# A rebuilt tail and a 512-column projection in a two-block transformer kernel on one Trainium2 core

## What is computed

```python
def second_block(x, g_mix, w_in, ..., w_e_gate, w_e_up, w_e_down, g_final):
    h = rmsnorm(x, g_mix[l])
    proj = h @ w_in[l]                       # queries, keys, values, gates of two attentions
    ...
    h = rmsnorm(x, g_ffn[l])
    x = x + hier_moe(h, ...)                 # 32 experts, 2 for each token
    return rmsnorm(x, g_final)

def hier_moe(h, ...):
    ...
    for e in range(N_EXPERTS):
        a = jax.nn.silu(hf @ w_e_gate[e]) * (hf @ w_e_up[e])
        out = out + gates[:, e:e + 1] * (a @ w_e_down[e])

def rmsnorm(x, gain):
    y = x32 * lax.rsqrt(jnp.mean(x32 * x32, axis=-1, keepdims=True) + RMS_EPS)
    return (y * gain).astype(x.dtype)
```

## Time and profile before

| | us |
|---|---|
| median of three runs | 1656.29 |
| the profiled execution | 1658.78 |
| its span, from first to last instruction | 1656.9 |
| TensorE busy | 1476.0 (89%) |
| VectorE, ScalarE, GpSimd busy | 766.9, 578.5, 462.3 |
| mean granted clock of TensorE | 0.954 of 2.4 GHz |

### The profile page before, as it was taken

One profiled execution on the slowest core, in us unless ns is written; L12 is line 12 of the kernel. 1 busy time (PEld: TensorE's weight loads), 2 busy tenths in 40 slices (PEclk: granted clock), 3 DMA queues, 4 the chain that ended last, 5 costly groups with the idle time before them and its releaser, 6 DMA issues.

```text
span 1656.9 us, 26936 instructions
## 1 busy us (share of the span) xinstructions
PE 1476.0 (89%) x10612; PEld 1176.3 (71%) x10612; DVE 766.9 (46%) x1476; ACT 578.5 (35%) x965; POOL 462.3 (28%) x257
## 2 busy tenths in 40 slices
PE   7999999999999999999999999999996666676665
PEld 6898998999999699889999998888942221131112
DVE  2665357777774274577776433768720000000002
ACT  2271444444453264444444333656410000000001
POOL 1332424555443142355555444212200000000000
PEclk9999999999999999999999999999998888778887
DMA  7464634555559443455552565243899999999994
GB/s 299 153 219 156 216 110 145 191 188 178 174 183 264 168 166 111 145 192 188 178 190 81 206 217 182 90 180 114 352 424 423 426 424 424 423 426 425 425 425 204
DMA packets 78691, 401.13 MB, mean 242 GB/s; under 512 B 8320, under 2 KB 13056, under 8 KB 67200
## 3 DMA queue, kind: packets, MB, share of 16 engines
q1 hardware_dynamic: 77584, 395.80, 64.6%
q10 hardware_dynamic: 1008, 3.94, 0.6%
HBM read 394.01 MB, written 1.05 MB: 238 GB/s over the span
## 4 chain that ended last, share of the span: by engine, by line
PE 64%; issue 28%; DVE 5%; ACT 1%; POOL 1%; DMA 0%; DVEq 0%; SPq 0%; POOLq 0%; ACTq 0%
PE pw L2097 10%; PE pw L2090 5%; PE pw L2099 5%; PE pw L2091 5%; PE pw L2092 5%; PE acc L2090 5%; PE acc L2091 4%; PE acc L2092 4%; PE pw L2413 4%; PE acc L2104 3%; PE acc L2273 2%; PE pw L2186 1%; PE pw L2235 1%; PE pw L2236 1%; PE pw L2237 1%
## 5 line engine op out<-in xcount | busy, mean ns | idle before, releaser
L1144 POOL TENSOR_TENSOR wl<-raw,wh 128x1024 fp32r<-128x1024 f32 x157 | 384.5, 2450 | 589.6 <-ACT wh L732 586.5
L732 ACT ACTIVATE wh<-raw 128x1024 fp32r<-128x1024 f32 x314 | 329.7, 1054 | 274.5 <-PE pw L2092 106.4
L2097 PE MATMUL pw<-a_pair,wh 128*128 128x512 f32 x720 | 256.8, 399 | 6.2 <-DVE cf L1598 3.3
L1261 DVE TENSOR_TENSOR wl<-raw,wh 128x1024 fp32r<-128x1024 f32 x157 | 203.7, 1298 | 108.9 <-ACT wh L732 108.7
L2099 PE MATMUL pw<-a_pair,wl 128*128 128x256 f32 x720 | 202.2, 281 | 0.0
L2090 PE MATMUL acc<-yh,wh 128*128 128x256 f32 x672 | 192.1, 286 | 0.5 <-DVE wl L1261 0.5
L2091 PE MATMUL acc<-yh,wl 128*128 128x256 f32 x672 | 190.1, 283 | 0.0
L2092 PE MATMUL acc<-yl,wh 128*128 128x256 f32 x672 | 190.1, 283 | 0.0
L2097 PEld LDWEIGHTS pw<-a_pair,wh 128*128 128x128 f32 x720 | 135.4, 188 | 38.4 <-DVE cf L1598 7.2
L2090 PE MATMUL pw<-a_pair,wh 128*128 128x256 f32 x552 | 159.5, 289 | 1.5 <-DVE gt L1770 1.5
L1155 POOL TENSOR_TENSOR small<-small 128x2 f32<-128x2 f32 x12 | 12.1, 1005 | 518.6 <-DVE small L1278 514.2
(11 more groups left out here) (354 smaller groups left out, 2438.6 us busy)
## 6 DMA issues: line engine op xcount, KB each, us to landing
raw<-in_stream SPq DMA_DIRECT2D x358, 512.0 KB, 3.4
raw<-in_experts SPq DMA_DIRECT2D x28, 2048.0 KB, 40.8
ring_w<-in_experts SPq DMA_DIRECT2D x18, 2048.0 KB, 33.4
ring_y<-in_experts SPq DMA_DIRECT2D x28, 1024.0 KB, 35.7
early_e<-in_experts SPq DMA_DIRECT2D x10, 2048.0 KB, 35.9
ring_a<-in_experts SPq DMA_DIRECT2D x10, 2048.0 KB, 36.1
ring_k<-in_experts SPq DMA_DIRECT2D x10, 2048.0 KB, 37.1
ring_b<-in_experts SPq DMA_DIRECT2D x10, 1024.0 KB, 34.0
```

The costliest lines, as they stand in the source:

```text
L732: A.done(act.activation(wh[:, s.base % SPLIT, :], raw[:, slot_of(s.base), :], ACT.Copy), w_hi)
L1144: G.done(pool.tensor_tensor(wl[:, s.base % SPLIT, :], raw[:, slot_of(s.base), :], wh[:, s.base % SPLIT, :].bitcast(F32), ALU.subtract), w_ ...
L1261: V.done(dve.tensor_tensor(wl[:, s.base % SPLIT, :], raw[:, slot_of(s.base), :], wh[:, s.base % SPLIT, :].bitcast(F32), ALU.subtract), w_lo_v)
L2097: pe.matmul(bank[:, 0:2 * T], wh[:, s.base % SPLIT, w], pair, start=start, stop=False, skip_group_check=True)
```

## The change

It has two parts.

In the **projection**, `col_phase` is called with `halves`, so the 29 slabs use `tile2`, and `col_out` scales the two halves (the low one into the scratch tile `t[1]`) and adds them.

In the **tail**, the last step becomes two: the last transfer is issued as two of 1 MB with a semaphore each (`last_in0`, `last_in1`), its weights lie in DRAM by halves, and each half brings what 128 output channels need. There are five steps `u`, with the chunks of `LAST`. Behind the products and the placing of a step `u` from 1 on, TensorE sums the squares of the step before (`out_sums`); VectorE adds two chunks behind the low part of a step (`take_experts`), and ScalarE squares them. The sums use a full 128 x 128 ones matrix and go to `pw2`, so that every partition holds the sums of all tokens. The flag of the branch is loaded ahead of the last steps, and the branch stands behind the additions on VectorE and behind the sums on TensorE; the dense form takes the additions back first. The column product, the copy, the diagonals and the spreading product go: VectorE scales the sums into `parts`, GpSimd raises all 128 x 256 of them to the power -1/2 into `rstd_b`, and the eight last multiplications read that from SBUF in place of PSUM.

```diff
@@ -50,6 +50,7 @@
+LAST = [(0, 2), (2, 4), (4, 6), (6, 7), (7, 8)]
@@ -549,6 +550,18 @@
+        def last_part(u):
+            lo, hi = LAST[u]
+            return pw[lo // 4][:, (lo % 4) * P:(lo % 4 + hi - lo) * P]
+        def last_slab(u, e, k):
+            m, n = EXPERT * QUADS - 4 + min(u, 3), LAST[u][1] - LAST[u][0]
+            if u < 3:
+                return expert_slab(m, e)[:, T * k:T * k + T]
+            return expert_place(m)[:, 2 * (u - 3) + e // 2, 512 * (e % 2) + P * k:512 * (e % 2) + P * k + P]
@@ -693,9 +706,13 @@
-            for m in range(FIRST, len(order)):
+            for m in range(FIRST, len(order) - 1):
+            wait_slab(sp, At(S0["moe"] + left_by(len(order) - 1)))
+            for h in range(2):
+                sp.dma_start(expert_place(len(order) - 1)[:, 2 * h:2 * h + 2, :],
+                             experts[order[-1], :, 2 * h:2 * h + 2, :]).then_inc(S(f"last_in{h}"), 16)
@@ -1071,13 +1088,22 @@
-            def y_hi_last(n):
-                wait_slab(act, At(NSLAB - 4 + n))
-                if n == 0:
+            def y_hi_last(u):
+                if u == 3:
+                    act.wait_ge(S("last_products"), 1)
+                else:
+                    wait_slab(act, At(NSLAB - 4 + min(u, 3)))
+                if u == 0:
-                A.done(act.activation(ye_hi[:, T * n:T * n + T], pw[n // 2][:, T * (n % 2):T * (n % 2) + T], ACT.Copy),
-                       S("expert_out_hi"))
+                lo, hi = LAST[u]
+                A.done(act.activation(ye_hi[:, P * lo:P * hi], last_part(u), ACT.Copy), S("expert_out_hi"))
+            def out_squares(u):
+                for c in range(*LAST[u]):
+                    wait_new_x(act, "moe", c)
+                    A.done(act.activation(sq_late[:, c, :], x[:, c, :], ACT.Square), sq_ready)
@@ -1114,10 +1140,14 @@
-            for n in range(4):
-                y_hi_last(n)
+            for u in range(5):
+                y_hi_last(u)
+                if 1 <= u < 4:
+                    out_squares(u - 1)
+            out_squares(3)
+            out_squares(4)
@@ -1246,7 +1279,9 @@
-            rstd("out")
+            pool.wait_ge(parts_ready, NORMS["out"] + 1)
+            G.fence()
+            G.done(pool.tensor_tensor(rstd_b[:], parts[:], mhalf[:, 0:1].broadcast_to([P, T]), ALU.pow), rstd_ready)
@@ -1337,6 +1369,8 @@
+                elif name == "win" and LEAD <= n < 32:
+                    ins = dve.tensor_tensor(dst, halves_scaled(pw[u % 4], t[1][:], scale), t[1][:], ALU.add)
@@ -2023,11 +2057,19 @@
-            def y_lo_last(n):
-                dve.wait_ge(S("expert_out_hi"), 2 * (QUADS - 1) + n + 1)
-                w = slice(T * n, T * n + T)
-                V.done(dve.tensor_tensor(ye_lo[:, w], pw[n // 2][:, T * (n % 2):T * (n % 2) + T],
-                                         ye_hi[:, w].bitcast(F32), ALU.subtract), S("expert_out_lo"))
+            def y_lo_last(u):
+                dve.wait_ge(S("expert_out_hi"), 2 * (QUADS - 1) + u + 1)
+                w = slice(P * LAST[u][0], P * LAST[u][1])
+                V.done(dve.tensor_tensor(ye_lo[:, w], last_part(u), ye_hi[:, w].bitcast(F32), ALU.subtract),
+                       S("expert_out_lo"))
+            def take_experts(lo):
+                dve.wait_ge(S("scattered"), QUADS - 1 + lo + 2)
+                V.fence()
+                for c in (lo, lo + 1):
+                    V.done(dve.tensor_tensor(x[:, c, :], acc_of(c), x[:, c, :], ALU.add), acc_out)
@@ -2051,11 +2093,18 @@
-            for n in range(4):
-                y_lo_last(n)
+            for u in range(5):
+                y_lo_last(u)
+                if 1 <= u < 4:
+                    take_experts(2 * u - 2)
+            take_experts(6)
+            V.fence()
...
@@ -2070,15 +2119,14 @@
-            V.fence()
-            take_sums("moe")
-            norm_parts("out")
-            norm_mean("out")
-            norm_diag("out")
-            dve.wait_ge(bc_full, spread_no("out"))
-            V.fence()
...
+            dve.wait_ge(stat_full, NORMS["out"] + 1)
+            V.done(dve.tensor_scalar(parts[:], pw[2][:, 0:T], 1.0 / D, EPS, ALU.mult, ALU.add), parts_ready)
+            dve.wait_ge(rstd_ready, NORMS["out"] + 1)
-                V.done(dve.scalar_tensor_tensor(x[:, c, :], x[:, c, :], col("g_final", c), acc[0][:, T:2 * T],
+                V.done(dve.scalar_tensor_tensor(x[:, c, :], x[:, c, :], col("g_final", c), rstd_b[:],
@@ -2484,7 +2532,7 @@
-            col_phase("win", 32 - LEAD, a_pair, spread_at("mix"), final_spread, 5, LEAD, LEAD)
+            col_phase("win", 32 - LEAD, a_pair, spread_at("mix"), final_spread, 5, LEAD, LEAD, True)
@@ -2718,15 +2766,12 @@
-            def scatter(q, chunks=range(KC)):
+            def scatter(q, chunks=range(KC), u=0):
-                if not ending:
-                    pe.wait_ge(S("expert_out_lo"), 2 * q + 2)
+                pe.wait_ge(S("expert_out_lo"), 2 * q + 1 + u if ending else 2 * q + 2)
-                    if ending and c % 2 == 0:
-                        pe.wait_ge(S("expert_out_lo"), 2 * q + 1 + c // 2)
@@ -2735,21 +2780,33 @@
+            def out_sums(u):
+                for c in range(*LAST[u]):
+                    pe.wait_ge(sq_ready, KC * sq_no("out") + c + 1)
+                    ins = pe.matmul(pw[2][:, 0:T], ones[:], sq_late[:, c, :], start=(c == 0), stop=(c == KC - 1))
+                    if c == KC - 1:
+                        ins.then_inc(stat_full, 1)
-                m = EXPERT * QUADS - 4
-                for n in range(4):
-                    wait_expert(pe, At(S0["moe"] + m + n))
+                for u in range(5):
+                    if u < 3:
+                        wait_expert(pe, At(NSLAB - 4 + u))
+                    else:
+                        pe.wait_ge(S(f"last_in{u - 3}"), 16)
-                            ins = pe.matmul(pw[n // 2][CAP * e:CAP * e + CAP, T * (n % 2):T * (n % 2) + T],
-                                            ht_last[:, k, CAP * e:CAP * e + CAP],
-                                            expert_slab(m + n, e)[:, T * k:T * k + T],
-                                            start=(k == 0 and n % 2 == 0), stop=(k == 3), skip_group_check=True)
-                    ins.then_inc(slab_done, 1)
-                    if n == 0:
+                            ins = pe.matmul(last_part(u)[CAP * e:CAP * e + CAP, :], ht_last[:, k, CAP * e:CAP * e + CAP],
+                                            last_slab(u, e, k), start=(k == 0 and u in (0, 2)), stop=(k == 3),
+                                            skip_group_check=True)
+                    ins.then_inc(S("last_products") if u == 3 else slab_done, 1)
+                    if u == 0:
-                    scatter(QUADS - 1, range(2 * n, 2 * n + 2))
+                    scatter(QUADS - 1, range(*LAST[u]), u)
+                    if u >= 1:
+                        out_sums(u - 1)
+                out_sums(4)
@@ -2804,10 +2861,11 @@
+            over = pe.value_load(overflow[0:1, 0:1], min_val=0, max_val=1)
-            over = pe.value_load(overflow[0:1, 0:1], min_val=0, max_val=1)
@@ -2833,9 +2891,10 @@
-            sq_sums("out", src=sq_late)
-            norm_column("out")
-            norm_spread("out")
...
@@ -2973,7 +3032,8 @@
-    experts = np.concatenate([experts, quarters])
+    halves = quarters[3].reshape(P, Q, 4, 2, P).transpose(0, 3, 1, 2, 4).reshape(1, P, Q, SLAB)
+    experts = np.concatenate([experts, quarters[:3], halves])
```

More of the change, by code:

```diff
@@ L1131, in _ @@
                             .then_inc(S("dense_turned"), 1)
-            squares(x, lambda c: wait_new_x(act, "moe", c), into=sq_late)
+                act.wait_ge(stat_full, NORMS["out"] + 1)
+                for c in range(KC):
+                    act.wait_ge(S("dense_added"), c + 1)
+                    act.activation(sq_late[:, c, :], x[:, c, :], ACT.Square).then_inc(S("dense_squares"), 1)
         @block.gpsimd
@@ L2053, in _ @@
             y_lo(QUADS - 2, 1)
-            for n in range(4):
-                y_lo_last(n)
             over = dve.value_load(overflow[0:1, 0:1], min_val=0, max_val=1)
+            for u in range(5):
[4 more added lines that the diff above has]
+            V.fence()
             with dve.If(over > 0):
-                dve.wait_ge(S("scattered"), QUADS - 1 + KC)
+                dve.wait_ge(sq_ready, KC * sq_no("out") + KC)
+                for c in range(KC):
+                    dve.tensor_tensor(x[:, c, :], x[:, c, :], acc_of(c), ALU.subtract).then_inc(S("dense_undone"), 1)
+                dve.wait_ge(S("dense_undone"), KC)
                 for q in range(TT):
@@ L2835, in _ @@
                 last.then_inc(S("dense_down"), 1)
-            sq_sums("out", src=sq_late)
-            norm_column("out")
-            norm_spread("out")
+                pe.wait_ge(S("dense_squares"), KC)
+                for c in range(KC):
+                    last = pe.matmul(pw[2][:, 0:T], ones[:], sq_late[:, c, :], start=(c == 0), stop=(c == KC - 1))
```

(1 more changed line is left out.)

9 lines of the change are left out of this document (5 added, 4 removed).

## The result

The changed kernel took 1692.97 us, the median of four runs (1691.5 to 1694.71), against 1655.78 us for the kernel before: a ratio of 1.023, with a 95% interval from 1.0218 to 1.0242. It is slower by 37 us, and outside the range of the prediction (1648 to 1680 us). The profiled execution took 1691.5 us around a span of 1689.7 us.

A forecast was written before the change was run, and what follows sets the result against it. Limits by stretch: matmuls in the projection, expert weights from 1169 us, a handover chain at the end. Projection -1.6, tail -5.75, power +4.7 give -2.65 us, median 1653.6 us, no measurable change; own range 1651 to 1661, outer range 1648 to 1680.

The forecast's parts named there:

- the price X: Tail: time of GpSimd's power of 256 columns, taken as 4.7 us between 1.4 and 54.
- The column rival: Tail: the power is paid by the column; at X = 27, +19.7 us, 1676 us, slower; chance 27%.
- deciding point of 12.3 us: Tail: the power's time X from which the column rival decides and the forecast of no measurable change fails.
- 0.6 + X: Tail, parts to last multiplications: parts 0.42 us, handovers about 0.18, and the power X, in place of 4.29 us.
- The term of the sums (-2.05 us): Tail: with most additions, squares and sums done before the last low part, the sums end 2.05 us earlier.
- The walk: Tail: turns priced one by one from quarter 1's placing at 1631.35 to the sums' end at 1644.7 us.
- the second transfer would gain no start: Tail: the first half lands 2.4 us earlier, but its products don't start before 1637.45, so no start is gained.
- The projection (-1.6 us): Input projection: 29 slabs, each 0.055 us shorter at 2.825 us in place of 2.88, give -1.6 us.
- should reach the end: From projection to end: what comes off the projection should reach the end, as each later stretch follows the one before.
- VectorE's 0.82 us: Tail, around the branch: VectorE's idle time ahead of the eight additions; moving the branch costed at nothing, at most 0.82 us.
- The clock rival: Tail: the end runs at 1.2 GHz, +3.3 us, 1656.9 us, no change; 5% together with the projection rival.
- VectorE didn't lag: Projection rival: VectorE lags and the 1.6 us are lost, 1655.2 us; 5% together with the clock rival.

The follow-up runs named there:

- column: The changed kernel with the factor made as in the kernel before (column product, power of two columns, diagonals, spreading product): 1654.63 us, ratio 0.9998.
- second profile: The kernel before, unchanged, profiled once more: 1653.44 us, one run.
- after: The changed kernel itself, against the kernel before: 1692.97 us, ratio 1.023.
- pow_split: The changed kernel with its GpSimd power of 128x256 written as four powers of 128x64: 1693.02 us, one run.
- pow_full: The changed kernel with the power's exponent read from a full 128x256 tile in place of one repeated column: 1694.2 us, one run.
- root: The changed kernel with the factor made by a square root on ScalarE and a reciprocal on VectorE: 1653.44 us, ratio 0.999.
- reorder: Against column: additions and squares right behind each step's own low and high part, its sums behind the next step's products: 1650.79 us, ratio 0.9972 to the kernel before.
- projection: The kernel before with the 512-column input projection alone: 1655.76 us, ratio 1.0002; 1654.34 us in the run for its second profile.

## Why the prediction was wrong

- **The step that failed is the price X.** The prediction bounded it between 1.4 us (all start) and 54 us (all by the column), and took 4.7, "a third of the way on a logarithmic scale". The rows gave no reason for that third. It is 41.1 us, 0.159 us a column, near the upper end: of the 0.69 us that the two-column row shows, some 0.32 are a start and most of the rest is the two columns. The likeness to the multiplication of the same shape on the same engine counted for nothing. The column rival, given 27%, was right, and X lies far beyond its deciding point of 12.3 us; at X = 27 it gave 1676, and the range ended at X = 31.
- **Its place was right.** Parts to last multiplications were predicted as 0.6 + X, and are 0.55 + 41.12. Nothing hid it: the run column, without it, is back at the time of the kernel before.
- **The term of the sums (-2.05 us) was too large, and had the wrong sign against the second profile.** The walk gave 13.35 us from the placing of quarter 1 to the end of the sums; after has 15.22, and so have pow_split, pow_full and root within 0.01. Each turn is some 0.45 us longer than walked: 2.04 us from placing to products in place of 1.60, then 4.93, 3.85 and 4.40 in place of 4.5, 3.35 and 3.9. A pair of sums by the full ones matrix holds TensorE 1.06 us, not 0.88. The rest is in the handovers: an addition's start is 0.46 us ahead of its square's, and that 0.47 ahead of its sum's (1631.94, 1632.40, 1632.87), where the prediction's prices are 0.34 each, an eighth of eight that follow each other. Against the profile that the prediction read, 15.22 is still a gain of 0.18 us; against its second profile (11.89) it is a loss of 3.33. The parts start 10.7 us after the last data (1642.21 and 1631.51), against 9.6 in the profile that the prediction read, where it expected some 2 us less.
- **The whole, counted from the second profile of the kernel before.** The placing of quarter 1 comes 1630.05 - 1626.96 = 3.09 us earlier, the sums take 3.33 more, and from their end to the last multiplications it is 41.70 in place of 1645.86 - 1641.94 = 3.92, 37.78 more. The sum is +38.0, and the spans are 1689.7 and 1651.7. With X at 41.1 the prediction's own terms would have given +33.8: the sums are 5.4 us worse than forecast, the start 1.5 better and the factor 0.4 worse.
- **Behind that term stands the order of the tail, as reorder shows.** There additions, squares and sums moved at once, and the sums end 1.35 us sooner after the placing than in the second profile of the kernel before. The prediction took the sums between two steps as given, and said that the second transfer would gain no start. That held (column), but the microsecond in which TensorE waits for squares could go into the pause for high and low part.
- **The projection (-1.6 us) came off in that size or more, and its way to the end was misjudged.** Slabs took 2.825 us, as predicted, in three executions (column, projection, pow_full) and 2.77 in the others. From its first row to that of its last slab the projection takes 81.86 us in the second profile of the kernel before, 80.21 and 79.04 in the two of the run projection: 1.6 or 2.8 us less. It reached the last data, which landed 1.8 us earlier in the first pair of profiles and 1.9 in the second. That it "should reach the end" failed in the kernel without the new tail, at TensorE's start behind the branch. The prediction had looked at VectorE's 0.82 us there, and not at TensorE. In after, the 3.09 us by which the placing comes earlier contain it; but in the kernels with the new projection and tail that placing starts anywhere from 1626.86 to 1629.56, so what is more than 1.9 may be this one execution's.
- **The clock rival** didn't come: the granted clock was 1.00 up to the end of the sums; it came in the run column, for the last sums alone, and cost 0.9 us there. VectorE didn't lag either; it waits for TensorE in every slab shown.

By the Trainium skill (GPSIMD Engine Reference, section 4.1 Engine selection) elementwise additions, multiplications and maxima belong on VectorE, as GpSimd is about twice as slow with two inputs. The multiplication in this trace agrees (0.99 us against 0.42). For the power, which that section doesn't list, the gap is far wider here: the same 128x256 factor takes 41.1 us as GpSimd's power, and 2.40 us by ScalarE and VectorE together. The Trainium skill's way to such a factor, VectorE's reciprocal with a ScalarE root (ScalarE: Activation LUTs, section What it computes), is what the run root does, there with the root first.

What stays open: why the run projection waits longer behind the branch than the kernel before (a code load fits, and is not proved), why the clock fell ahead of the last sums in the run column and not in after, and why slabs take 2.77 us in some executions and 2.825 in others.

## What to carry to other kernels

A duration known only at two columns says little of the duration at 256: where bounds lie 40 times apart and the operation would stand alone at the end of the chain, measure one wider instance first, or give the upper end its weight. Widening an operation to save handovers pays only if its cost by the column is known to be small; here 254 more columns of a power cost 40 us and the handovers that went were worth 3.7. Before walking a tail from one profile, look whether that execution was an ordinary one (its time against the median, waits for data, clock), and in an in-order queue put work that waits for another engine into a pause, not ahead of work that is ready.

## What the runs showed of the hardware

- GpSimd's power costs 0.159 us a column of 128 partitions and 0.32 us of start (64 columns 10.52 us, 256 columns 41.12), whether its second operand is repeated or full.
- VectorE's reciprocal of 128x256 took 1.75 us, four times the 0.42 us of its other operations on this shape; a root on ScalarE took 0.47.
- With the projection's other form (a third of its products less on TensorE, two instructions a slab more on VectorE) TensorE started 2.6 and 2.9 us later behind a jump 650 us on, in the two profiles of that program. A packet on the instruction queue lay in each of these waits, and the longer wait had the longer packet by the same 0.35 us.
